# One decoder trunk on one Trainium2 core: the first down projection split by experts with the next pair's transposes between them, and half of the second down projection ahead of the first scatter

## What is computed

```python
scores = sigmoid(x @ router_w)              # 64 experts, 8 chosen per token
for each expert e, on its tokens xb with gate wt:
    hb = silu(xb @ w_gate[e]) * (xb @ w_up[e])      # 1024 -> 256
    y[tok] += (hb @ w_down[e]) * wt                 # 256 -> 1024
y += (silu(x @ s_gate) * (x @ s_up)) @ s_down       # shared expert
```

## Time and profile before

| | |
|---|---|
| runs (3) | median 1263.84 us, 1263.64 to 1265.28 |
| the profiled execution | 1263.44 us; its span 1261.8 us, so 1.6 us lie around the span |
| mean granted TensorE clock | 0.988 of full |
| busy, share of the span | PE 96%, PEld 45%, DVE 32%, ACT 23%, POOL 2% |
| traffic | 447.72 MB, mean 355 GB/s |
| chain that ended last | PE 86%, DVE 6%, DMA 4%, ACT 2%, issue 1% |

### The profile page before, as it was taken

How to read it: one execution, slowest core, us unless ns; L and a number is a source line. 1 busy time by engine, 2 the same in 40 slices (tenths; PEclk the granted TensorE clock), 3 DMA queues, 4 the chain that set the end, 5 groups by cost and what they waited for, 6 DMA issues and landing times.

```text
span 1261.8 us, 17152 instructions
## 1 busy us (share of the span) xinstructions
PE 1205.8 (96%) x6960; PEld 564.0 (45%) x6960; DVE 399.4 (32%) x892; ACT 295.2 (23%) x651; POOL 30.3 (2%) x106
## 2 busy tenths in 40 slices
PE   8998999999999999999979999999999999999995
PEld 5776753434343434434336565343434343443431
DVE  3667373212221212222144556321222121222214
ACT  3354331212121212212112343121212121221112
POOL 1005000000000000000000000000000000000000
PEclk9999999999999999999989999999999999999998
DMA  9408068999999999999992646799999999999993
GB/s 369 164 16 326 4 272 361 394 426 427 429 427 427 429 429 426 428 428 427 427 378 81 267 200 279 288 387 425 429 429 428 426 427 427 427 430 426 431 426 147
DMA packets 45024, 447.72 MB, mean 355 GB/s; under 512 B 8096, under 2 KB 9504, under 8 KB 18848
## 3 DMA queue, kind: packets, MB, share of 16 engines
q1 hardware_dynamic: 44368, 446.29, 84.7%
q10 hardware_dynamic: 592, 0.53, 0.2%
HBM read 445.75 MB, written 1.05 MB: 354 GB/s over the span
## 4 chain that ended last, share of the span: by engine, by line
PE 86%; DVE 6%; DMA 4%; ACT 2%; issue 1%; DVEq 0%; SPq 0%; ACTq 0%
PE psum L411 33%; PE psum L516 17%; PE psum L497 5%; PE psum L427 5%; PE psum L2384 4%; DMA w_up_ring<-in_moe_up 4%; PE psum L2239 4%; PE psum L1264 3%; PE psum L476 2%; PE psum L614 2%; PE psum L648 1%; PE psum L2390 1%; PE psum L1743 1%; PE psum L1571 1%; DVE moe_h L1097 1%
## 5 line engine op out<-in xcount | busy, mean ns | idle before, releaser
L411 PE MATMUL psum<-w_up_ring,moe_x_selected 128*64 128x512 f32 x2048 | 452.4, 593 | 5.8 <-DMA w_up_ring<-in_moe_up 5.7
L411 PEld LDWEIGHTS psum<-w_up_ring,moe_x_selected 128*64 128x64 f32 x2048 | 149.4, 137 | 295.7 <-issue 286.1
L516 PE MATMUL psum<-w_down_ring,moe_hT 128*64 128x512 f32 x960 | 221.2, 603 | 0.0
L1097 DVE SCALAR_TENSOR_TENSOR moe_h<-moe_silu,moe_slot_gate,psum 128x256 f32<-128x256 f32 x64 | 30.7, 480 | 382.5 <-ACT moe_silu L846 382.2
L846 ACT ACTIVATE moe_silu<-psum 128x256 f32<-128x256 f32 x64 | 24.7, 385 | 430.1 <-PE psum L411 430.1
L516 PEld LDWEIGHTS psum<-w_down_ring,moe_hT 128*64 128x64 f32 x960 | 65.7, 138 | 125.4 <-issue 108.8
L1102 DVE TENSOR_TENSOR moe_out_low<-psum,moe_out_high 128x512 fp32r<-128x512 f32 x64 | 44.3, 692 | 226.5 <-ACT moe_out_high L858 226.5
L858 ACT CAST moe_out_high<-psum 128x512 fp32r<-128x512 f32 x64 | 37.5, 586 | 130.6 <-PE psum L516 130.6
L497 PE MATMUL psum<-moe_out_high,moe_matchT 32*128 32x512 f32 x496 | 62.7, 496 | 3.5 <-DVE moe_out_low L1104 3.5
L1104 DVE TENSOR_TENSOR moe_out_low<-psum,moe_out_high 128x512 fp32r<-128x512 f32 x64 | 44.2, 691 | 63.5 <-ACT moe_out_high L860 63.5
L427 PE MATMUL psum<-moe_match,moe_x_high 128*128 128x256 f32 x224 | 60.8, 307 | 2.8 <-ACT moe_x_selected L835 2.8
(11 more groups left out here) (538 smaller groups left out, 1072.3 us busy)
## 6 DMA issues: line engine op xcount, KB each, us to landing
w_up_ring<-in_moe_up SPq DMA_DIRECT2D x128, 2048.0 KB, 15.3
w_down_ring<-in_moe_down SPq DMA_DIRECT2D x60, 2048.0 KB, 15.2
w_up_ring<-in_ev_columns SPq DMA_DIRECT2D x4, 2048.0 KB, 17.4
w_up_ring<-in_od_w_in SPq DMA_DIRECT2D x4, 2048.0 KB, 17.6
w_up_ring<-in_ev_out SPq DMA_DIRECT2D x2, 2048.0 KB, 8.0
moe_first_down<-in_moe_down SPq DMA_DIRECT2D x2, 2048.0 KB, 10.0
w_up_ring<-in_od_w_out SPq DMA_DIRECT2D x2, 2048.0 KB, 7.7
ln_gain_bias<-in_ln_g SPq DMA_DIRECT2D x4, 512.0 KB, 6.7
```

The source lines that it names most:

```text
L411: last = nc.tensor.matmul(k.psum[e * SLOTS:(e + 1) * SLOTS, 6, :], xsel[:, kk, own:own + SLOTS], up_view(par, e, kk), start=kk == 0, stop= ...
L516: last = nc.tensor.matmul(k.psum[e * SLOTS:(e + 1) * SLOTS, bank, :], hT[:, j * P + e * SLOTS:j * P + (e + 1) * SLOTS], places[e][:, j, ha ...
L1097: nc.vector.scalar_tensor_tensor(h[:], silu[:], slot_gate[:, i:i + 1], up_ps[:, FE:2 * FE], ALU.mult, ALU.mult).then_inc(s.h, 1)
```

## The change

It touches `first_two_pairs` and ACT's order beside it. In both layers:

```diff
@@ output_and_experts @@
+    def pe_first_down(e, half):
+
+        for j in range(KF):
+            last = nc.tensor.matmul(k.psum[e * SLOTS:(e + 1) * SLOTS, (4, 7)[half], :], hT[:, j * P + e * SLOTS:j * P + (e + 1) * SLOTS],
+                                    first_down[:, e, j, half * BANK:(half + 1) * BANK], start=j == 0, stop=j == KF - 1)
+        return last
+
@@ first_two_pairs @@
             pe.wait_ge(s.turned_sb, 1)
             pe.wait_ge(x.dn_first, 16)
-            pe_down([first_down[:, 0], first_down[:, 1]], 0, 4).then_inc(s.down_a, 1)
-            pe_down([first_down[:, 0], first_down[:, 1]], 1, 7).then_inc(s.down_b, 1)
+            pe_first_down(0, 0)
+            pe_first_down(0, 1)
+            pe.wait_ge(s.h, 2)
+            pe_turn().then_inc(s.turned, 1)
+            pe_first_down(1, 0).then_inc(s.down_a, 1)
+            pe_first_down(1, 1).then_inc(s.down_b, 1)
             pe_turn_match().then_inc(s.match_turned, 1)
-            pe.wait_ge(s.shared_h, 1)
-            pe.wait_ge(s.h, 2)
-            pe.wait_ge(s.matchT, 1)
             pe.wait_ge(s.low_a, 1)
-            pe.wait_ge(s.low_b, 1)
-            pe_combine(0, 0, begin=True).then_inc(s.half_combined, 1)
-            pe_turn(early=True).then_inc(s.turned, 1)
-            pe.wait_ge(s.half_combined, 1)
-            pe_combine(0, 1).then_inc(s.combined, 1)
             pe.wait_ge(s.turned_sb, 2)
             pe.wait_ge(dn[1], 16)
             pe_down(k.w_down[2:4], 0, 4).then_inc(s.down_a, 1)
+            pe.wait_ge(s.shared_h, 1)
+            pe.wait_ge(s.matchT, 1)
+            pe.wait_ge(s.low_b, 1)
+            pe_combine(0, 0, begin=True).then_inc(s.half_combined, 1)
+            pe.wait_ge(s.half_combined, 1)
+            pe_combine(0, 1).then_inc(s.combined, 1)
             pe_down(k.w_down[2:4], 1, 7).then_inc(s.down_b, 1)
@@ scalar @@
-        take_high(0, whole=True)
+        take_high_a(0)
+        act.wait_ge(s.down_b, 1)
+        take_turned(1)
+        take_high_b(0)
         take_match(0)
         act.wait_ge(s.table_sb, 1)
         act.dma_start(k.over_dram, table_i[:]).then_inc(s.table_dram, 16)
-        take_turned(1, early=True)
+        act.wait_ge(s.combined, 1)
         take_high(1)
```

More of the change, by code:

```diff
@@ L854, in take_match, with take_high_a, take_high_b, take_high @@
             nc.scalar.copy(matchT[:].rearrange("p i n -> p (i n)"), k.psum[:, 5, :]).then_inc(s.matchT, 1)
-        def take_high(p, whole=False):
-            act.wait_ge(s.down_b if whole else s.down_a, p + 1)
+        def take_high_a(p):
+            act.wait_ge(s.down_a, p + 1)
             nc.scalar.copy(high[:, 0:BANK], k.psum[:, 4, :]).then_inc(s.high_a, 1)
+        def take_high_b(p):
             act.wait_ge(s.down_b, p + 1)
             nc.scalar.copy(high[:, BANK:], last_ps).then_inc(s.high_b, 1)
+        def take_high(p):
+            take_high_a(p)
+            take_high_b(p)
         def pair(q, i, final=False):
```

## The result

| | before | the change |
|---|---|---|
| median of 20 runs each | 1263.21 us (1259.96 to 1265.28) | 1265.61 us (1264.07 to 1268.07) |
| ratio | | 1.0018, 95% interval 1.0011 to 1.0024 |
| profiled execution | 1263.44 us, span 1261.8, clock 0.988 | 1265.02 us, span 1263.2, clock 0.990 |

By the ratio the change costs 2.3 us (1.4 to 3.0); the medians lie 2.4 apart. The 0.18% is inside the 0.2% that I called no difference, though the interval reaches over it, and the sign is not in doubt. The page's chain is PE 86%, DVE 5%, DMA 4%; only DVE's share, by one point, is not what it was.

The account below looks back on a forecast made before the run. Transfers and TensorE nearly balance, with the weight stream restarting after pair 1's down projection. Per layer 3.43 and about 0.4 us added, 1.77 idle and 1.6 to 1.7 slow clock removed: +1.1, 1264.5 us (1264.9 against the median), range 1260.8 to 1268.7.

Parts of the forecast that it names:

- The row of the full array: Profile row for 128-column matmuls, 0.44 us each; from it a lone 64-column record was put at 0.43 us.
- the half in front: Half of pair 1's down projection before the scatter: 1.82 us, to cover the copies and splitting with 0.7 us to spare.
- the turn: Pair 1's transposes between the two experts' runs in the first down projection: 0.31 us.
- The bare `half_combined`: Wait between the two scatter steps with nothing in it: 0.11 us, so 0.67 + 0.11 + 0.67 for the scatter.
- about 0.4: Per layer, us for the rest of the wait, one more change of shape and the bare `half_combined`.
- ACT's table transfer: On ACT's queue the table's transfer goes out about 5 us later, with 4 us left before it is needed.
- The sum: Stretch from first down projection to next up projection: +0.6 us in layer 0, +0.5 in layer 1, together +1.1 us.
- the slow clock: Half clock from the scatter's start to the next up projection, costing 1.6 and 1.7 us, removed by the change.
- The clock falls all the same: Rival, 18%: the clock still falls in the changed stretches, the old 1.6 + 1.7 us loss returns, 1268.2 us.
- Expert 1 doesn't pay: Rival, 10%: lone 64-column records take 0.215 us or expert 1 runs beside expert 0 in the first down projection; 1258.2 us.
- The end doesn't move with the restart: Rival, 10%: transfers catch up within the layer, so TensorE's 0.6 us vanishes in later waits; 1263.8 us.
- Full value: Every shift of pair 1's down projection end was counted whole at the layer's end, twice, once per layer.

Follow-up runs that it names:

- the copy: The kernel before, run again with nothing edited: 1264.28 us, ratio 1.0003 to the kernel before.
- The filled gap: The kernel before with two unused float32 matmuls of 448 columns put where TensorE idles ahead of the first scatter: 1261.55 us, ratio 0.9982 to the kernel before.
- the alternating kernel: The change with the first down projection's records alternating between the experts again, transposes between its output-column halves: 1259.43 us, ratio 0.9964 to the kernel before.
- the late restart: The change with SP's down refill also waiting for the middle of pair 2's up projection: 1269.97 us, ratio 1.0054 to the kernel before.
- the second group: Runs on the second chip, kernel before at 1263.56 us; the change, repeated there with nothing edited: 1265.98 us, ratio 1.0021.
- the first part alone: The change with pair 0's scatter ahead of both halves of pair 1's down projection again: 1268.95 us, ratio 1.0043 to the kernel before.

## Why the prediction was right, and where it was off

**The two mechanisms hold, by experiments that change one of them at a time.** A run of one expert's 64-column matmuls costs as much as both experts' together: 3.52 us for eight records against 1.82 when they alternate. The row of the full array, 0.44 us a matmul, was the right neighbour. And the half in front covers the splitting: `low_b` was over 0.75 us before the scatter, where 0.7 was forecast.

**The timeline, step by step (layer 0):**

| start of | predicted | measured |
|---|---|---|
| turn of pair 1 | 211.55 | 211.54 |
| expert 1 | 211.86 | 211.91 |
| match transposes | 215.40 | 215.49 |
| first half of pair 1's down projection | 216.03 | 216.07 |
| scatter | 217.85 | 217.93 |
| second half | 219.30 | 219.41 |
| next up projection | 221.02 | 221.18 |

The term that was most off is the turn: 0.37 us here, not the 0.31 of the earlier trace rows. The bare `half_combined` took 219.41 - 217.93 = 1.48 us with both steps, against 1.45. These two make 0.09 us of the 0.15 by which the stretch (13.16 instead of 13.01) is longer; the rest is spread over the other steps. Two side figures of the prediction were off without effect: its sum in words has "about 0.4" us for the small terms where its own timeline has 0.56 (13.01 us less 10.79 at full clock, less 3.43, plus 1.77), and ACT's table transfer went out 3.9 us later (215.93 against 211.99), not 5.

**The sum** was +1.1 us and is +1.4 in the traces. Against the medians it is +2.3. The term that was mis-sized is the slow clock. It was entered as a certain saving of 1.6 and 1.7 us; its measured price in that trace, 1.50 and 1.63, is about right, but the fall is not in every execution, and the median of the kernel before holds only a part of it. By the copy's 10.89 us the change costs 13.16 - 10.89 = 2.27 us per layer, 4.5 in all, where no fall is saved. The filled gap puts the falls' worth in the median at 2.0 us (1263.58 - 1261.55; 1.1 to 3.4 by its interval). That leaves 2.5 (1.1 to 3.4), and 2.3 was measured.

**The rivals.** *The clock falls all the same*: no, in four stretches of two traces of the change it is at 1.00. Its time, 1268.2, was not reached. *Expert 1 doesn't pay*: no, by the alternating kernel, 3.40 us per layer. The rule of the Trainium skill's page "TensorEngine Tiling (Array Packing)", section "Key Properties", that different tiles can execute in parallel, is not contradicted: sixteen alternating records take the time of eight. But expert 1's matmuls, behind the transposes, did not start beside expert 0's: 13.16 us for the stretch against 9.76. Strict alternation is not what it takes. In the mixer of the kernel before, the attention's matmuls on 64 columns (`L1330`) stand in the code two by two, four records on one half of the array's columns and then four on the other:

```profile
93.95 2.18 PE L1330 MATMUL psum<-even_pT,even_v 128*64 128x128 f32 x32
...
741.37 0.38 PE L2456 MATMUL psum<-odd_mqT,odd_mkT 128*128 128x128 f32 x2
741.59 0.60 PE L2455 MATMUL psum<-odd_mqT,odd_mkT 128*128 128x256 f32 x2
```

They take 2.18 / 32 = 0.07 us a record, where a record of the same length on the full array takes (741.59 - 741.37) / 2 = 0.11. So runs of four still overlap in good part. Whether in the change the runs of eight or the transposes between them keep the two experts apart wasn't tried. *The end doesn't move with the restart*: no, by the late restart, though a delay is passed on only in part (4.4 of 6.9 us). Full value was right enough for a shift that TensorE and the transfers make together: from the first down projection to the last scatter the four layers of the change's two traces take 440.95 to 441.53 us, 441.25 in the mean. That is 0.8 more than the profiled kernel before (440.43 and 440.44), for a stretch that is 0.7 longer, and 2.5 more than the copy without a fall (438.73 and 438.74), for 2.27.

The chance of slower by over 0.2% was 20%, for a clock that falls. The measured 0.18% stands just short of that bound, by another cause. So the forecast of no difference came true with some luck: the loss is twice the +1.1 us of the sum, and the second group measured 0.21%, beyond the bound.

## What to carry to other kernels

Here, eight records on half of the array's columns, parted by transposes from the eight on the other half, cost the time of the full array; alternating, they cost half. To free something early, look for another axis along which to split such work, as here by output columns, so that both halves keep alternating: that made 3.4 us per layer of difference, and turned a loss of 0.2% into a gain of 0.3 to 0.4%. Work that is moved into a wait is worth the idle that it fills, less what the move costs: 1.1 us here, for an idle of 1.44. Now and then it also saves a slow clock that the wait would bring. Before a clock fall goes into a sum at full price, look at a second execution of the same kernel; a mean clock alone doesn't say where the falls were.

## What the runs showed of the hardware that was not expected

The same instruction stream, with the same 1.77 us of idle, had the granted clock at half (1.2 GHz) behind it in one execution (2 of 2 layers) and full in another (2 of 2 layers, and a fall at 126 us in the mixer instead). In the first part alone, one execution had both: half in layer 0, full in layer 1, behind equal gaps of 1.44 us. A fall cost 1.50 to 1.70 us. The Trainium skill's page "TensorE: Matmul & The Clock Gate", section "Part 1: The HAM clock gate", says of the rise of the clock that its point varies from run to run of one kernel. These traces agree as far as they go, and show it for falls too, by the 126 us of the one and the 214 us of the other. With an idle of 0.21 us or less, no fall was seen in any of the 16 stretches profiled.
